# Merge and output projection in three reduced-precision passes, with gate chunks and two attention products moved

## The reference

```python
def merge_branches(y_a, y_b, g_logits, w_pa, w_pb, w_o):
    g_a, g_b = jnp.split(g_logits, 2, axis=-1)
    mixed = jax.nn.sigmoid(g_a) * (y_a @ w_pa) + jax.nn.sigmoid(g_b) * (y_b @ w_pb)
    return mixed @ w_o
```

## Time and profile before

| | |
|---|---|
| median of 3 runs | 2036.67 us |
| the profiled execution's own time | 2035.58 us |
| its span, first to last instruction | 2033.8 us |
| PE matmul busy | 1947.2 us, 96% of the span |
| DVE busy | 729.7 us, 36% |
| ACT busy | 610.7 us, 30% |
| POOL busy | 397.0 us, 20% |
| mean granted TensorE clock | 0.98 of full |

### The profile page before, as it was taken

The page is one execution under the profiler, slowest core; times in us unless marked ns, Lnnn a source line. Parts: engine busy times, 40 slices in busy tenths (PEclk is TensorE's granted clock), DMA queues, the critical chain, the costliest instruction groups (busy, mean ns, idle before and its releaser), DMA issues.

```text
span 2033.8 us, 27449 instructions
## 1 busy us (share of the span) xinstructions
PE 1947.2 (96%) x11522; PEld 1405.9 (69%) x11522; DVE 729.7 (36%) x1209; ACT 610.7 (30%) x931; POOL 397.0 (20%) x209
## 2 busy tenths in 40 slices
PE   5999999999999999997999899999999999988998
PEld 2777786864444444445787657777777778778998
DVE  1625243232222222226243754222222445474333
ACT  2523002032222222223111534322223511445454
POOL 2000000020000000005000521433333310334664
PEclk9999989989999999998999999999999999999999
DMA  9469717549999999983222202544444223414551
GB/s 357 160 246 354 289 42 269 192 166 387 429 424 424 425 422 424 425 356 114 84 101 95 86 31 93 194 149 145 147 172 157 85 83 124 168 42 149 183 180 49
DMA packets 120213, 428.38 MB, mean 211 GB/s; under 512 B 5690, under 2 KB 23141, under 8 KB 107456
## 3 DMA queue, kind: packets, MB, share of 16 engines
q1 hardware_dynamic: 118016, 416.56, 53.1%
q0 software_dynamic: 2112, 10.57, 1.4%
HBM read 426.07 MB, written 1.05 MB: 210 GB/s over the span
## 4 chain that ended last, share of the span: by engine, by line
PE 63%; PEld 20%; issue 7%; DVE 3%; POOL 2%; ACT 2%; DMA 2%; PEldq 1%; DVEq 0%; POOLq 0%; SPq 0%; ACTq 0%
PE bank L527 61%; PEld bank L527 19%; PE bank L542 2%; DMA ring<-in_ada_w 2%; DMA ring<-in_w_in 1%; PEldq L506 0%; POOL arena L1823 0%; POOL arena L1822 0%; DVE H L1914 0%; DVE H_low L1921 0%; POOL arena L1825 0%; DVE arena L2409 0%; POOL arena L1827 0%; POOL arena L1828 0%; POOL arena_r L1869 0%
## 5 line engine op out<-in xcount | busy, mean ns | idle before, releaser
L527 PE MATMUL bank<-arena_r 128*128 128x512 f32 (+1 forms) x2112 | 599.0, 350 | 11.2 <-ACT arena_r L1340 5.4
L527 PE MATMUL bank<-arena_r,ring_low 128*128 128x512 f32 (+2 forms) x1792 | 561.3, 347 | 5.4 <-DVE H_low L1921 5.3
L527 PEld LDWEIGHTS bank<-arena_r 128*128 128x128 f32 x2112 | 374.0, 190 | 103.6 <-issue 46.2
L527 PEld LDWEIGHTS bank<-arena_r,ring_low 128*128 128x128 f32 (+1 forms) x1792 | 328.9, 189 | 51.4 <-issue 6.1
L527 PE MATMUL bank<-arena 128*128 128x64 bf16 (+8 forms) x2588 | 309.6, 285 | 26.4 <-DMA arena<-in_hy_filt_w 11.8
L527 PEld LDWEIGHTS bank<-arena 128*128 128x128 bf16 (+4 forms) x2588 | 190.7, 132 | 130.8 <-issue 98.0
L527 PE MATMUL bank<-ring,arena 128*64 128x512 f32 x1024 | 278.2, 595 | 1.1 <-ACT arena L1509 0.7
L527 PE MATMUL bank<-H_low,arena_r 128*128 128x512 f32 (+1 forms) x672 | 216.5, 339 | 0.0
L2465 DVE SCALAR_TENSOR_TENSOR X<-bank,mod,X 128x256 f32<-128x256 f32 x216 | 94.7, 479 | 314.2 <-PE bank L527 314.0
L1354 ACT ACTIVATE arena<-bank 128x512 f32<-128x512 f32 (+2 forms) x106 | 51.4, 497 | 404.9 <-PE bank L527 404.9
L1855 POOL TENSOR_TENSOR ring_low<-ring,arena_r 128x2048 fp32r<-128x2048 f32 x32 | 146.9, 4613 | 127.0 <-ACT arena_r L1699 71.4
(11 more groups left out here) (287 smaller groups left out, 1982.4 us busy)
## 6 DMA issues: line engine op xcount, KB each, us to landing
ring<-in_moe_w_gate SPq DMA_DIRECT2D x32, 2048.0 KB, 13.4
ring<-in_w_mlp SPq DMA_DIRECT2D x32, 2048.0 KB, 8.8
ring<-in_w_in SPq DMA_DIRECT2D x26, 2048.0 KB, 8.1
ring<-in_ada_w SPq DMA_DIRECT2D x24, 2048.0 KB, 11.8
ring<-in_moe_w_up SPq DMA_DIRECT2D x17, 2048.0 KB, 9.0
H<-in_moe_w_down SPq DMA_DIRECT2D x16, 2048.0 KB, 15.8
arena<-in_moe_w_up SPq DMA_DIRECT2D x15, 2048.0 KB, 9.1
ring<-in_moe_w_down SPq DMA_DIRECT2D x15, 2048.0 KB, 15.9
```

The lines of the kernel that those rows point to most:

```text
L527: ins = nc.tensor.matmul(o, l, r, start=start, stop=stop, skip_group_check=True)
```

## The change

1. Merge and output projection go from one float32 `mm` per k-step to `mm3`. ACT copies the high halves of the four chunks (`merge_high`, two copies of 2048 columns per chunk) and DVE subtracts the low halves (`merge_low`, two pieces per chunk). `merge_high(0)` stands between the gate tiles of ACT's queue, `merge_high(1)` behind a wait for `y_spec` 2 and ahead of the last two gate tiles, `merge_high(2)` ahead of the barrier "hyena", `merge_high(3)` behind it. `merge_low` of chunk 0 stands behind the products of `spectrum_half(0)`, of chunk 1 behind those of `spectrum_half(1)`, of chunk 2 behind the barrier and after mixing tile 4, of chunk 3 after mixing tile 7 and after `out_added` 2.
2. `OS`, `YB` and each tile of `MIX` are split by DVE: one more copy and one more subtraction each.
3. `take_chunk` and `gains` move from ahead of the barrier to behind the mixing.
4. The chunk order: `win(10)` becomes chunk WIN + 27 and the third modulation chunk WIN + 28; PE calls `ada(GATE_ADA[2])` after the four tiles of gate chunk 10, and `ada(GATE_ADA[3])` after `spectrum_half(0)`.
5. In both attention phases `gate_queries(d)` moves from POOL to DVE, for d = 0 behind `gate_args(1)` and for d = 1 behind `gate_products(1)`; POOL keeps the clears. Semaphore counts follow (left out below where nothing else changes).

```diff
-            return WIN + j + sum(len(b) for b in BEHIND[:j]) if j < 8 else WIN + (23, 24, 28, 30)[j - 8]
-        GATE_ADA = [WIN + 25, WIN + 26, WIN + 27, WIN + 29, WIN + 31]
+            return WIN + j + sum(len(b) for b in BEHIND[:j]) if j < 8 else WIN + (23, 24, 27, 30)[j - 8]
+        GATE_ADA = [WIN + 25, WIN + 26, WIN + 28, WIN + 29, WIN + 31]
...
-        MT = A3(17408, KT, L)
+        MT = mrow[0].rearrange("p (a b) -> p a b", a=2)
+        OSh, YBh = AR3(1024, HYT, L), AR3(2048, HYT, L)
+        OSl, YBl = AR3(0, HG_H, L), AR3(12288, HYT, L)
+        MIXh, MIXl = AR3(17408, KT, L), AR3(15360, KT, L)
+        MERGEh = [[flat[:, 0:2048], flat[:, 2048:4096]] for flat in (Hl[:, :, :].rearrange("p k n -> p (k n)"), ar_r[:, 21504:25600])]
+        MERGEh += [[ar_r[:, 8192:10240], ar_r[:, 13312:15360]], [ar_r[:, 10240:12288], ar_r[:, 19456:21504]]]
...
             ada(GATE_ADA[1], 6, 6, 1, 5)
-            ada(GATE_ADA[2], 6, 6, 2, 5)
             for nt in range(2):
                 gate_tile(10, nt)
...
             chunk_used()
-            ada(GATE_ADA[3], 6, 6, 3, 5)
+            ada(GATE_ADA[2], 6, 6, 2, 5)
             pe.wait_ge(S("un_ready"), 2)
             spectrum_half(0)
+            ada(GATE_ADA[3], 6, 6, 3, 5)
...
             def merge(nt, side):
+                c = slice(nt * P, (nt + 1) * P)
+                wl = as_rows(MERGE + side, slot=low)
+                high, lower = ((OSh, OSl), (YBh, YBl))[side]
                 for k in range(4):
-                    mm(ps[nt % 4][:, side * L:(side + 1) * L], as_rows(MERGE + side)[:, k, nt * P:(nt + 1) * P], (OS, YB)[side][:, k, :],
-                       k == 0, k == 3, "merge_mm" if (side, k) == (1, 3) else None)
-            chunk_in(MERGE)
+                    wh = MERGEh[side][k // 2].rearrange("p (k n) -> p k n", k=2)
+                    mm3(ps[nt % 4][:, side * L:(side + 1) * L], (wh[:, k % 2, c], wl[:, k, c]), (high[:, k, :], lower[:, k, :]),
+                        k == 0, k == 3, "merge_mm" if (side, k) == (1, 3) else None)
+            pe.wait_ge(S("w_split"), 5 + 1)
...
-            chunk_in(MERGE + 1)
+            pe.wait_ge(S("w_split"), 5 + 2)
...
+                wh = MERGEh[2 + t // 4][k // 4].rearrange("p (k n) -> p k n", k=4)
+                mm3(ps[4 + t % 2][:, 0:L], (wh[:, k % 4, c], as_cols(n, slot=low)[:, k, c]), (MIXh[:, k, :], MIXl[:, k, :]),
+                    k == 0, k == KT - 1, "out_mm" if k == KT - 1 else None)
...
+            def merge_high(m):
+                act.wait_ge(full[(MERGE + m) % RING], arrived(MERGE + m))
+                for a in range(2):
+                    A_(MERGEh[m][a], slot(MERGE + m)[:, 2048 * a:2048 * (a + 1)], ACT.Copy).then_inc(S("high_copied"), 1)
             gate_tiles(10, 2)
-            gate_tiles(12, 4)
+            merge_high(0)
+            gate_tiles(12, 2)
+            act.wait_ge(S("y_spec"), 2)
+            merge_high(1)
+            gate_tiles(14, 2)
             ada_rows(6, 6, 0)
+            merge_high(2)
             phase_end(act, "hyena")
+            merge_high(3)
...
-                def gate_queries(d):
-                    pool.wait_ge(S("g_exp"), 3 * (2 * l + d) + 3)
-                    G.tensor_tensor(GQD[d][:, :, 0:W], GQD[d][:, :, 0:W], GQ[:, :, 0:W], ALU.mult).then_inc(S("gsc_clear"), 1)
...
+            link(V.tensor_copy(OSh, OS))
+            V.tensor_tensor(OSl, OS, OSh.bitcast(F32), ALU.subtract)
+            def merge_low(m, a):
+                c = slice(2048 * a, 2048 * (a + 1))
+                dve.wait_ge(S("high_copied"), 2 + 2 * m + a + 1)
+                i = V.tensor_tensor(low(MERGE + m)[:, c], slot(MERGE + m)[:, c], MERGEh[m][a].bitcast(F32), ALU.subtract)
+                if a:
+                    i.then_inc(S("w_split"), 1)
...
                 dve.drain().then_inc(S("y_spec"), 1)
+                merge_low(f, 0)
+                merge_low(f, 1)
...
             link(V.tensor_tensor(YB, UV, CV[:, 8:12, :], ALU.mult))
+            link(V.tensor_copy(YBh, YB))
+            V.tensor_tensor(YBl, YB, YBh.bitcast(F32), ALU.subtract)
+            phase_end(dve, "hyena")
+            merge_low(2, 0)
+            for nt in range(KT):
+                dve.wait_ge(S("merge_mm"), nt + 1)
+                o = ps[nt % 4]
+                V.tensor_tensor(MIX[:, nt, :], GL[:, nt, :], o[:, 0:L], ALU.mult)
+                link(V.tensor_tensor(MT[:, nt % 2, :], GL[:, 8 + nt, :], o[:, L:2 * L], ALU.mult))
+                link(V.tensor_tensor(MIX[:, nt, :], MIX[:, nt, :], MT[:, nt % 2, :], ALU.add))
+                link(V.tensor_copy(MIXh[:, nt, :], MIX[:, nt, :]))
+                V.tensor_tensor(MIXl[:, nt, :], MIX[:, nt, :], MIXh[:, nt, :].bitcast(F32), ALU.subtract).then_inc(S("merged"), 1)
+                if nt == 4:
+                    merge_low(2, 1)
+            merge_low(3, 0)
             take_chunk(1, 6, 6, 28, 5)
...
                                        ALU.mult, ALU.add).then_inc(S("out_added"), 1)
+                if t == 1:
+                    merge_low(3, 1)
...
+                def gate_queries(d):
+                    dve.wait_ge(S("g_exp"), 3 * (2 * l + d) + 3)
+                    V.tensor_tensor(GQD[d][:, :, 0:W], GQD[d][:, :, 0:W], GQ[:, :, 0:W], ALU.mult).then_inc(S("gq_ready"), 1)
...
                 gate_args(1)
+                gate_queries(0)
                 gate_states(0)
                 end_product(1)
                 gate_products(1)
+                gate_queries(1)
                 gate_masks(1, 0)
```

More of the change, by code:

```diff
@@ L287, in _ @@
                 load(n, cols(T["w_in"], WIN_ORDER[j] * 512, 512), as_cols(n))
-                for i in BEHIND[j] if j < 8 else ([], [15, 16, 17], [18], [19])[j - 8]:
+                for i in BEHIND[j] if j < 8 else ([], [15, 16], [17, 18], [19])[j - 8]:
                     n += 1
@@ L832, in merged_out @@
                 n = MERGE + 2 + t // 4
-                mm(ps[4 + t % 2][:, 0:L], as_cols(n)[:, k, (t % 4) * P:(t % 4 + 1) * P], MIX[:, k, :], k == 0, k == KT - 1,
-                   "out_mm" if k == KT - 1 else None)
-            chunk_in(MERGE + 2)
+                c = slice((t % 4) * P, (t % 4 + 1) * P)
+                wh = MERGEh[2 + t // 4][k // 4].rearrange("p (k n) -> p k n", k=4)
+                mm3(ps[4 + t % 2][:, 0:L], (wh[:, k % 4, c], as_cols(n, slot=low)[:, k, c]), (MIXh[:, k, :], MIXl[:, k, :]),
+                    k == 0, k == KT - 1, "out_mm" if k == KT - 1 else None)
+            pe.wait_ge(S("w_split"), 5 + 3)
             for k in range(KT):
@@ L842, in _ @@
                 if t == 4:
-                    chunk_in(MERGE + 3)
+                    pe.wait_ge(S("w_split"), 5 + 4)
                 pe.wait_ge(S("out_added"), t - 1)
@@ L1127, in g_scores @@
                     g = 2 * l + d
-                    pe.wait_ge(S("gq_ready"), g + 1)
+                    pe.wait_ge(S("gq_ready"), 2 * g + 1)
                     if part and nx == 4:
@@ L1171, in _ @@
                 g_intra(0, 1)
-                pe.wait_ge(S("gsc_clear"), 4 * l + 2)
+                pe.wait_ge(S("gq_ready"), 4 * l + 2)
                 g_inter(0)
@@ L1179, in _ @@
                 g_intra(1, 1)
-                pe.wait_ge(S("gsc_clear"), 4 * l + 4)
+                pe.wait_ge(S("gq_ready"), 4 * l + 4)
                 g_inter(1)
@@ L1281, in mlp_pair @@
                                 n += 1
-                        pe.wait_ge(S("w_split"), 5 + 8 * l + j + 1)
+                        pe.wait_ge(S("w_split"), 9 + 8 * l + j + 1)
                         for nt, ks in [(t, (0, 1, 2)) for t in range(3)] + [(t, (3,)) for t in range(3)] + [(t, (0, 1, 2, 3)) for t in range(3, KT)]:
@@ L2113, in _ @@
             V.tensor_tensor(lbc[:, 0:8], vec("fin", 0, 8), vec("fin", 0, 8), ALU.mult)
-            phase_end(dve, "hyena")
-            for nt in range(KT):
-                dve.wait_ge(S("merge_mm"), nt + 1)
-                o = ps[nt % 4]
-                V.tensor_tensor(MIX[:, nt, :], GL[:, nt, :], o[:, 0:L], ALU.mult)
-                link(V.tensor_tensor(MT[:, nt, :], GL[:, 8 + nt, :], o[:, L:2 * L], ALU.mult))
-                V.tensor_tensor(MIX[:, nt, :], MIX[:, nt, :], MT[:, nt, :], ALU.add).then_inc(S("merged"), 1)
             for t in range(KT):
@@ L2315, in _ @@
                         s = slice(2048 * a, 2048 * (a + 1))
-                        dve.wait_ge(S("high_copied"), 4 + 2 + a + 1)
+                        dve.wait_ge(S("high_copied"), 12 + 2 + a + 1)
                         i = V.tensor_tensor(low(n)[:, s], slot(n)[:, s], NEXTh[2 + a].bitcast(F32), ALU.subtract)
@@ L2472, in _ @@
                 for a in range(2):
-                    dve.wait_ge(S("high_copied"), 2 + 6 * l + a + 1)
+                    dve.wait_ge(S("high_copied"), 10 + 6 * l + a + 1)
                     i = V.tensor_tensor(YTl[a][:, :, 0:W], YT[:, 4 * a:4 * a + 4, 0:W], YTh[:, 4 * a:4 * a + 4, 0:W].bitcast(F32), ALU.subtract)
@@ L2500, in mlp_pair @@
                                 s = slice(2048 * a, 2048 * (a + 1))
```

(2 more changed lines are left out.)

4 lines of the change are left out of this document (1 added, 3 removed).

## The result

The changed kernel takes 2015.96 us (median of 5 runs, 2015.12 to 2018.08), the kernel before 2036.67 (2035.01 to 2044.7) in the same comparison. The ratio is 0.9894 with an interval of 0.9878 to 0.991, so the gain is 18 to 25 us, about 21. The forecast, 2020.6 from a gain of 16.1 us, has the direction and nearly all of the mechanism, but its gain is too small, and the time stands at the low end of its range, 2015.5: the median lies 0.5 us inside, and by the ratio, 0.9894 x 2036.67 = 2015.1, it lies just outside.

A forecast was written before the change was run, and what follows sets the result against it. PE was taken as the bound, with matmuls and weight loads holding 83% of the chain. The terms 4.33 + 9.3 - 0.2 + 2.7 = 16.1 us, taken from 2036.67, gave 2020.6 us, range 2015.5 to 2026.5.

The forecast's parts named there:

- Gate chunk order: First gate tiles: PE's 2.54 us load wait and 1.79 us of slow clock go, 4.33 us gained; bounds 2.5 and 4.3.
- Three passes: Merge and output: 128 k-steps at 0.36 us in place of 0.433, 9.3 us gained.
- the first addition: Output: PE's tile 2 waits for tile 0's addition to X, after DVE's mixing; 0.2 us lost.
- Dearer passes, the rival: Merge and output: weight loads show, 0.57 us per k-step, 17.5 us lost in place of 9.3 gained, time 2047; 3%.
- The halves: Ahead of inverse and merge: high and low weight halves ready before PE wants them; late-halves rival 2025.4 us, 14%.
- margin of 1.2 us: Ahead of the inverse: `y_spec` 2 ready at 350.7, PE wants it at 351.9; called the thinnest place.
- A mixed tile: DVE's mixing before output: 1.21 us plus two added operations of 0.42, 2.05 us per tile.
- Attention: Both attention phases: moving products to DVE ends contention with POOL, 2.7 us gained; rival that it gives nothing, 2023.3 us, 6%.
- worth up to 1.5 us more: Attention layer 0: a shorter PE wait may keep the clock up; left out of the sum, rival at 2019.0 us, 14%.
- Layer 1: Attention layer 1: products of 512 columns on DVE add 0.61 us, line 2402 gets shorter; 0.45 us gained.
- The range: Whole kernel: 2015.5 to 2026.5 us, from clock kept up in both stretches to late halves with a clock fall.

The follow-up runs named there:

- pool_dummy: The changed kernel with one GpSimd product of 1024 columns on zeros added in attention layer 0, where the second product stood; 2019.16 us, ratio 0.9908.
- no_gate_order: The changed kernel with the old gate chunk order; 2022.56 us, ratio 0.9931.
- after_look_a: The changed kernel itself, unchanged, one more profiled execution; 2019.78 us.
- after_look_c: The changed kernel itself, unchanged, one more profiled execution; 2017.48 us.
- after_look_b: The changed kernel itself, unchanged, one more profiled execution; 2014.05 us.
- double_low0: The changed kernel with one more VectorE operation of 2048 columns ahead of the last subtraction of weight chunk 0; 2015.99 us, ratio 0.9894.
- att_only: The kernel before with only the two attention products moved to VectorE; 2033.06 us, ratio 0.9989.
- before_look_c: The kernel before itself, unchanged, its fifth profile; 2033.45 us.
- gate_only: The kernel before with only the new gate chunk order; 2031.1 us, ratio 0.9985.
- after_again: The changed kernel itself, run again unchanged; 2015.47 us, ratio 0.9895.
- one-edit kernels: The kernel before with one edit alone: gate chunk order 2031.1 us, attention products on VectorE 2033.06 us, three passes with their halves 2026.32 us.
- before_again: The kernel before itself, run again unchanged; 2035.08 us, ratio 1.0003.

## Why the prediction was right, and where it was wrong

**Gate chunk order: right.** 4.33 us forecast, 3.96 in the profile, 4.1 between the means. Both parts are as told: the wait of 2.54 us goes, and the clock stays at 1.00, in all ten profiles with the new order. The clock's part is 1.69 (8.86 - 7.17) and not 1.79, and the records of the stage take 0.27 us more in their new order, which the sum left out. The forecast took 2.54 us of wait and the fallen clock for fixtures. In eight profiles of the old order the wait is 2.26 to 3.56 us, and the clock stayed up in the two shortest (2.26 and 2.36), so the term is 2.0 to 5.0 us, by the execution (53.40 and 56.38 us from the first ada call to the merge, 51.40 in the new order).

**Three passes: right to a tenth.** 0.36 us per k-step and 9.3 us forecast, less 0.2 for the first addition; 9.11 measured, and 9.11 given back with float32 steps in the trace (their median is 8 us above the changed kernel's). The Trainium skill's figure of 262 cycles for an isolated 256-column matmul, section Back-to-back issue gap of "TensorE: Matmul & The Clock Gate", gives 0.33 per k-step by the forecast's estimate; the trace has 0.36 and decides. Dearer passes, the rival, are out: 0.36 us per k-step in place of 0.57.

**The halves: right.** Forecast were the landing 12.3 us behind the issue (12.4), `y_spec` 2 at 350.7 and PE's want at 351.9; taking off the 5.6 us by which the profile was ahead before, that is 345.1 and 346.3, and measured are 345.4 and 346.5. The margin of 1.2 us is there (1.17), and one piece of 2.28 us more turned it into a wait of 1.43. A mixed tile takes 1.91 us and not 2.05, since the copy of 256 columns costs 0.29 us and not 0.42; so DVE was never late at the additions.

**Attention: the contention right, the clock put at nothing.** This is the step that failed: 2.7 us forecast, 4.8 in the profile that was compared (3.93 + 0.83), 3.9 between the means. The waits of layer 0 came as priced (-1.27, +1.02 and -2.16 beside -1.27, +1.14 and -2.14), and pool_dummy shows contention as their cause. What the forecast left out of its sum was the clock, "worth up to 1.5 us more", which stood among the rivals with 14%. Measured it is 1.52 us in the compared profile, and a gain of this size came in six of nine. In the eight profiles with GpSimd's products the clock fell within 1.4 us after the start of PE's matmuls behind the wait, and in pool_dummy inside the wait; with VectorE's products alone it fell there in none of nine. What takes 1.4 us back in three of the nine (no_gate_order, after_look_a, after_look_c: 2.55 us in layer 0 in place of 3.9) is another fall, about 3 us ahead of the wait, that lasts past it. What brings that one is not known. In after_look_b and double_low0 it came too, was over by the wait or within 0.2 us of PE's start, and cost under 0.1. Layer 1 is no miss: 0.83 in the compared profile, 0.5 between the means, beside 0.45 forecast. PE's wait of 1.71 us went to nothing there because PE itself came late at a low clock (1.78 us for eight records that take 1.09); in after_look_b it is 0.64.

**The range: too narrow for what the clock does in code that no edit touches.** The forecast's profile held four spells in the scans, 6.6 us, and the changed kernel's own profile one. They are draws: 0 to 4 in five profiles of the kernel before, 0 to 3 in five of the changed one. From 421 to 485 us, too, the changed kernel was mostly 1.3 us shorter, by a lower share of slow clock; att_only and before_look_c don't have it, gate_only does. Whether the edits bring that by where they move this stage, or chance does, is not settled.

Of the 4.6 us by which the median lies below the forecast, 2.1 are in the means of the profiles (18.2 us beside 16.1): 1.2 from attention's clock, 0.9 from 421 to 485, and the rest cancels. The other 2.5 stay open: the means of profiled executions are 18.2 us apart, the medians 20.7 in the result and 21.0 beside after_again, with runs that scatter by 8 us (changed) and 18 us (before). The medians of the three one-edit kernels sum to less, 14.8 us. The runs without a profile can't be divided into stages.

## What to carry to other kernels

Read a stage's price from several profiles of the same kernel before it goes into a sum: the scans' 6.6 us, the 1.7 us behind the wait on `w_in` and the 1.4 us in attention were draws of the clock, and one profile couldn't tell them from properties of the code. Here a wait of 2.54 us cost 1.69 us more in what followed when the clock fell; a sum that shortens such a wait should hold both outcomes, each with its chance. Where VectorE and GpSimd run products on SBUF side by side, count the one that starts second as waiting for the first (3.36 us for 1.22 here): a product moved onto the busier engine can shorten its path.

## What the runs showed of the hardware

The clock fell at one or another of the four places in the same code: near 236 us in before_again, near 272 and from 289 to 299 us in the forecast's profile, and nowhere in the scans in before_look_c. Ahead of it PE had done the same work in the same time as where it didn't fall: the stretch before, in before_again and in gate_only, whose clock then stayed at 1.00:

```profile
228.00:232.00 4.00, 3.50 (x32) 3.43 (x32) 1.69 (x3) 0.57 (x2) 0.00 (x0) 1.00 1.06 388
```

```profile
228.00:232.00 4.00, 3.50 (x33) 3.44 (x32) 1.59 (x3) 0.85 (x2) 0.00 (x0) 1.00 1.05 388
```

Products of 1024 columns on SBUF, VectorE's and GpSimd's, took turns: the later one's row was longer by the wait, whichever engine it was (3.36 for 1.22 us on VectorE, 3.33 and 3.43 for 2.37 on GpSimd).

A VectorE copy to fp32r of 256 columns takes 0.29 us, of 1024 columns 0.69, beside 0.42 and 1.22 for an arithmetic operation with two inputs.
